# Seven-product matrix sets in a two-layer block: the weight sums of even and odd sets change engines, and two norm steps move

## The reference, cut to what matters

```
for l in range(2):
    n = rms_norm(h, mix_norm_g[l])
    proj = n @ w_in[l]                    # q, k, v, indexer, rnn, conv, gates
    ... attention, recurrent and convolution branches, merged ...
    h = h + merged @ w_out[l]
    f = rms_norm(h, ffn_norm_g[l])
    a = silu(f @ w_ffn_gate[l]) * (f @ w_ffn_up[l])     # width 2816 = 22 tiles of 128
    h = h + a @ w_ffn_down[l]
return h[:, 16:]
```

## Time and profile before

| | us |
|---|---|
| median of 3 runs | 1786.79 (1786.48 to 1790.79) |
| profiled execution | 1786.79 |
| its span | 1785.0 |
| TensorE busy | 1737.6 (97%) |
| VectorE busy | 953.5 (53%) |
| ScalarE busy | 492.0 (28%) |
| GpSimd busy | 326.7 (18%) |

### The profile page before, as it was taken

The page is one execution under the profiler, slowest core; times in us unless marked ns, Lnnn a source line. Parts: engine busy times, 40 slices in busy tenths (PEclk is TensorE's granted clock), DMA queues, the critical chain, the costliest instruction groups (busy, mean ns, idle before and its releaser), DMA issues.

```text
span 1785.0 us, 32239 instructions
## 1 busy us (share of the span) xinstructions
PE 1737.6 (97%) x13478; PEld 1442.2 (81%) x13478; DVE 953.5 (53%) x1921; ACT 492.0 (28%) x1064; POOL 326.7 (18%) x349
## 2 busy tenths in 40 slices
PE   6999998899899999999999999999999999999999
PEld 3345654898877888888889999988888888899999
DVE  2225335566456857566325765348667563257643
ACT  2122236344343124742102100051146322020100
POOL 0002300564100000000003555200000000036652
PEclk9999999799999999999999999999999999999999
DMA  8322300000234433332443444443334334444453
GB/s 326 121 94 95 118 24 1 3 4 4 95 145 142 142 142 133 127 127 109 142 141 142 166 166 154 158 161 142 142 135 145 122 118 142 152 155 168 171 170 107
DMA packets 53360, 225.46 MB, mean 126 GB/s; under 512 B 5088, under 2 KB 29024, under 8 KB 29280
## 3 DMA queue, kind: packets, MB, share of 16 engines
q1 hardware_dynamic: 53216, 223.40, 35.0%
HBM read 222.34 MB, written 1.05 MB: 125 GB/s over the span
## 4 chain that ended last, share of the span: by engine, by line
PE 93%; DVE 3%; ACT 2%; issue 1%; DMA 1%; DVEq 0%; SPq 0%; ACTq 0%
PE PS L535 26%; PE PS L730 14%; PE PS L676 13%; PE PS L1926 9%; PE PS L754 8%; PE PS L1423 2%; PE PS L1436 2%; PE PS L548 1%; PE PS L2024 1%; PE PS L649 1%; PE PS L694 1%; PE PS L688 1%; DMA ring<-stream_dram 1%; PE PS L618 1%; PE PS L630 1%
## 5 line engine op out<-in xcount | busy, mean ns | idle before, releaser
L535 PE MATMUL PS<-arena,ring 128*128 128x272 f32 (+1 forms) x2176 | 498.1, 389 | 0.0
L535 PEld LDWEIGHTS PS<-arena,ring 128*128 128x128 f32 x2176 | 411.2, 190 | 77.2 <-issue 1.4
L676 PE MATMUL PS<-arena,ring 128*128 128x272 f32 (+1 forms) x1024 | 229.5, 386 | 2.1 <-DVE arena L1210 2.1
L995 DVE SCALAR_TENSOR_TENSOR arena<-arena,par 128x272 f32<-128x272 f32 (+1 forms) x480 | 214.8, 488 | 16.7 <-issue 1.3
L676 PEld LDWEIGHTS PS<-arena,ring 128*128 128x128 f32 x1024 | 194.2, 190 | 36.0 <-DVE arena L1210 2.9
L954 POOL TENSOR_TENSOR arena<-ring 128x512 f32<-128x512 f32 (+1 forms) x32 | 39.9, 1246 | 978.0 <-PE PS L688 927.1
L1926 PE MATMUL PS<-arena,ring 128*128 128x512 f32 (+2 forms) x448 | 158.3, 514 | 1.7 <-DVEq L2241 1.7
L730 PE MATMUL PS<-arena 128*128 128x136 f32 (+1 forms) x1280 | 152.1, 277 | 0.0
L730 PEld LDWEIGHTS PS<-arena 128*128 128x128 f32 x1280 | 148.7, 191 | 0.0
L1926 PEld LDWEIGHTS PS<-arena,ring 128*128 128x128 f32 (+1 forms) x448 | 84.0, 189 | 75.1 <-issue 69.6
L769 ACT ACTIVATE arena<-PS 128x272 f32<-128x272 f32 (+1 forms) x144 | 55.5, 392 | 320.4 <-PE PS L535 313.9
(11 more groups left out here) (361 smaller groups left out, 2297.1 us busy)
## 6 DMA issues: line engine op xcount, KB each, us to landing
ring<-stream_dram SPq DMA_DIRECT2D x185, 1024.0 KB, 4.8
ring<-stream_dram SPq DMA_DIRECT2D x32, 512.0 KB, 4.3
ring<-stream_dram SPq DMA_DIRECT2D x16, 384.0 KB, 3.7
arena<-x_dram SPq DMA_DIRECT2D x1, 2048.0 KB, 11.4
cst<-const_dram SPq DMA_DIRECT2D x1, 1080.0 KB, 7.9
out_dram<-H SPq DMA_DIRECT2D x4, 256.0 KB, 3.4
cst<-const_dram SPq DMA_DIRECT2D x1, 912.0 KB, 9.6
arena<-stream_dram SPq DMA_DIRECT2D x1, 512.0 KB, 7.6
```

Of the source, the lines that this page charges most:

```text
L535: last = mm(PS[:, (m + f) % 4, nw], lslot(l, n, KD, 256)[:, k, P * f:P * f + P], NT[:, k, nw], start=k == 0, stop=k == KD - 1)
L676: last = mm(PS[:, i % 4, NQ], lslot(l, n, KD, 256)[:, k, P * (i % 2):P * (i % 2) + P], src[:, k, NQ], start=k == 0, stop=k == KD - 1)
L995: stt(CVG[:, c, NQ], CVA[:, c, j + Q0:j + T2], dw_w[l][:, c, j:j + 1], CVG[:, c, NQ], ALU.mult, ALU.add)
```

## The change

Three edits. First, in layer 1 (not in layer 0) the norm sum of the first norm is issued behind tile m = 0. Second, the seven `add_square` steps go, and one `add_tiles` (which waits for all eight squares) takes their place. Third, GpSimd and VectorE exchange their parts: VectorE makes the sums of the even sets, GpSimd those of the odd ones, each at the places in its list where its former sums stood.

```diff
                 if m == 0 and l == 0:
                     pe.wait_ge(fn_added, 1)
                     sum_parts(SQF, 4, slice(META, T2), fn_sums)
-                if m == 1:
+                if m == (0 if l else 1):
                     norm_sums(0, 5, NW)
...
-            def add_square(k):
-
-                dve.wait_ge(L["sq"], B["sq"] + KD + k + 1)
-                dr()
-                return tt(SQS[:, NQ], SQ2[:, 0, NQ] if k == 1 else SQS[:, NQ], SQ2[:, k, NQ], ALU.add)
...
                     tt(H[:, f, NQ], H[:, f, NQ], made, ALU.add).then_inc(L["br_kept"], 1)
-                    if f > 1:
-                        add_square(f - 1)
-            add_square(KD - 1).then_inc(L["added"], 1)
+            dve.wait_ge(L["sq"], B["sq"] + 2 * KD)
+            add_tiles(v, SQS[:, NQ], SQ2[:, :, NQ], SQ2[:, 0:4, NQ]).then_inc(L["added"], 1)
...
-            def odd_sums(j):
+            def even_sums(j):
...
-                weight_sums(v, quarters(l, FF_S + 2 + j), WS[j % 4]).then_inc(L["odd_sums"], 1)
+                weight_sums(v, quarters(l, FF_S + 2 + j), WS[j % 4]).then_inc(L["even_sums"], 1)
...
-            odd_sums(1)
+            even_sums(0)
             for j in range(QUADS):
...
                 if j % 2 == 0:
-                    odd_sums(j + 3)
+                    even_sums(j + 2)
...
-                for s in ((3, 5), (7,), (9, 11), ())[fp]:
-                    odd_sums(QUADS + s)
+                for s in ((2, 4), (6,), (8, 10), ())[fp]:
+                    even_sums(QUADS + s)
...
-            def even_sums(j):
+            def odd_sums(j):
...
-                weight_sums(g, quarters(l, FF_S + 2 + j), WS[j % 4]).then_inc(L["even_sums"], 1)
+                weight_sums(g, quarters(l, FF_S + 2 + j), WS[j % 4]).then_inc(L["odd_sums"], 1)
...
             for p in range(FT // 2):
-                even_sums(2 * p)
+                odd_sums(2 * p + 1)
...
-            for s in range(2, DOWNS, 2):
-                even_sums(QUADS + s)
+            for s in range(3, DOWNS, 2):
+                odd_sums(QUADS + s)
```

## The result

The changed kernel took 1807.7 us in the median of 5 runs (1799.0 to 1808.3), the kernel before 1786.79 (1783.04 to 1790.79). The ratio is 1.0102, with an interval of 1.0073 to 1.0131, which is 18.2 us (13.0 to 23.4); forecast were 16.9. The median itself lies 0.7 us above the upper end of the stated range. Run a second time, beside other kernels, the same code took 1801.81 us against 1786.85, ratio 1.0088 (1.0072 to 1.0103), which is 15.7 us (12.9 to 18.4).

What follows compares the result with a forecast made beforehand. TensorE, busy 97% of the span, was taken to bound the kernel. Waits of 2.65 + 4.68 + 5.06 = 12.4 us plus 4.5 us of slow clock on 1786.8 gave 1803.7 us; 8-of-10 range 1798.5 to 1807.

Steps and rivals of the forecast that it cites:

- Whatever newly makes TensorE wait is paid in full.: Rule for the whole kernel: new TensorE waits cost their full length; relieving other engines pays nothing unless TensorE waited for it.
- First norm of layer 1: At layer 1's start, TensorE waits 2.65 us for the squares' sum, and all of layer 1 starts that much later.
- the earlier root: In layer 1's first norm the root comes 0.8 us sooner, helping nobody: VectorE idles until ScalarE's swap.
- Squares: At the second norm the three-step sum exceeds its cover: 0.84 us of new waiting in layer 0, 0.88 in layer 1.
- Exchange, set 0: At set 0's third product TensorE waits for VectorE's late sums: 3.84 and 4.18 us, besides the second norm's 0.84 and 0.88.
- The 0.3 us allowed for this: Allowance, either way, for GpSimd's new sums of set 1 shifting VectorE's products: 0.3 us.
- Other sets: Sets after the first cost nothing: 1.4 us to spare in layer 1, 3.5 left in the down projection.
- The rival of late sums: VectorE late in every other set, each step waiting out a GpSimd step: 0.5 us in nine layer 1 sets, 1808.2 us; chance 0.11.
- Clock: Granted clock falls to half behind the three longest new waits: 1.6 us at each set 0, 1.3 at layer 1's start, together 4.5.
- A fall that was counted at 1.3: Clock fall behind the 2.65 us wait at layer 1's first norm, taken between two earlier cases: 1.3 us.
- The sum: Whole kernel: 12.4 us of waiting plus 4.5 us of slow clock, 16.9 us, giving 1803.7 us.
- Early sums cost nothing: Rival: set 0's sums run in VectorE's idle time before the root, 4.4 us in all, 1791.2 us; chance 0.05 with other no-cost ways.

Runs made afterwards that it cites:

- split wait: Kernel before, with the output projection's tile waiting for the last merged tile only at its eighth matmul: ratio 0.9993; same edit on the kernel with set 0 ahead: 1.0003.
- exchange alone: Kernel before with only the third edit, VectorE summing the even sets and GpSimd the odd: ratio 1.0085 (1.0066 to 1.0104).
- control: The changed kernel run again without any edit, against the kernel before: 1801.81 us, ratio 1.0088 (1.0072 to 1.0103).
- the kernel with set 1 later: The exchange alone, with GpSimd's sums for set 1 moved behind its first token sums: ratio 1.0032 (1.0020 to 1.0045) to the kernel before.
- the kernel with set 0 ahead: The exchange alone, with VectorE making set 0's sums before waiting for the second norm's root: ratio 0.9997 (0.9981 to 1.0014) to the kernel before.

## Why the prediction was right

Point by point, by its own steps; shifts are differences between the same loads of the two profiles.

- *"Whatever newly makes TensorE wait is paid in full."* Held to 0.3 us for every edit alone, the falls of the clock aside, and with the other sign for the split wait.
- *First norm of layer 1.* Forecast 2.65 us, measured a wait of 2.66 on the loads, and L562 2.5 us later. VectorE's idle time ahead of L1051 grew from 9.66 to 13.11 us, so the earlier root ended in an idle engine:

```profile
1197.06 1.23 DVE L1051 TENSOR_TENSOR arena<-arena 128x1024 f32<-128x1024 f32 x1 [13.11 <-ACT arena L801]
```

- *Squares.* Forecast 0.84 and 0.88, measured 0.81 and 0.83 of idle loads; the first up tile came 0.65 and 0.70 us later.
- *Exchange, set 0.* Forecast waits of 3.84 and 4.18 us, measured 4.05 and 4.39. The step was right, its size 0.2 short: beside GpSimd's token sums VectorE's four steps took what they had taken (0.68 to 0.96 us each), but VectorE's products ahead of them took 5.04 us in place of 4.67. The 0.3 us allowed for this was too small for the exchange alone, where it was 0.8.
- *Other sets.* Forecast 1.4 us to spare in set 4 of layer 1. Measured: sums end at 1628.69 + 0.69 = 1629.38, third product loaded at 1631.23, 1.85 to spare. In the changed kernel, VectorE and then the loads:

```profile
1623.84 1.42 DVE L954 TENSOR_TENSOR arena<-ring 128x512 f32<-128x512 f32 x1
1625.19 1.75 DVE L955 TENSOR_TENSOR arena<-ring 128x512 f32<-128x512 f32 x1
1627.02 1.60 DVE L957 TENSOR_TENSOR arena<-arena,ring 128x512 f32<-128x512 f32 x1
1628.69 0.69 DVE L959 TENSOR_TENSOR arena<-ring,arena 128x512 f32<-128x512 f32 x1
```

```profile
1631.23 0.86 PEld L730 LDWEIGHTS PS<-arena 128*128 128x128 f32 x7
```

  GpSimd's steps of the same time:

```profile
1623.45 1.27 POOL L955 TENSOR_TENSOR arena<-ring 128x512 f32<-128x512 f32 x1
1624.86 1.53 POOL L957 TENSOR_TENSOR arena<-arena,ring 128x512 f32<-128x512 f32 x1
1626.53 1.54 POOL L959 TENSOR_TENSOR arena<-ring,arena 128x512 f32<-128x512 f32 x1
```

  The rival of late sums was rightly rejected, but the prediction's reason for it, that VectorE is held up by less than a GpSimd step each time, needs a closer look. L954, L955 and L957 of VectorE end at 1625.26, 1626.94 and 1628.62, each 0.55 us behind the end of the GpSimd step during which it began (1624.72, 1626.39, 1628.07). So each is held until that step ends. The sum is 5.5 us and not 7.8 because each begins 0.3 to 0.5 us into the GpSimd step, so that less than a whole step is left to wait, and because the fourth, L959, met none and took 0.69.
- *Clock.* Forecast 4.5 us by three falls. In the profile there were two and no third; the same 2.3 us wait had one in three of the other kernels and none in the control. At set 0 both came each time. A fall that was counted at 1.3 stayed away, while the one at layer 1's set 0 lasted twice 3.41 us.
- *The sum.* Forecast 2.65 + 1.72 + 8.02 + 4.5 = 16.9 us. By the lengths of the parts the profile gives 2.5 for the first norm, 1.35 for the squares, 8.4 for the waits at set 0, 0.5 of restart behind them (the kernel with set 1 later, whose clock stayed up, shows 0.24 us a layer on top of its waits), for which the prediction had no term, and so 3.8 for the clock: 16.6. The mechanism was right, but that the totals lie 0.3 us apart is in part luck, as the waits came out longer and the norms and the clock cheaper.
- *Early sums cost nothing.* Rightly excluded for this kernel, and right as a mechanism, as the kernel with set 0 ahead shows.

## What to carry to other kernels

When two engines exchange alternate jobs, look at the first job of each list, not at the steady state: the steady state had room for the exchange in 31 of 32 sets, and the one job that lost an idle stretch to run in cost 13 us in two layers. Put work that an engine can do with what has already landed ahead of its next wait, and split a wait so that only the last matmul needs the last input. Where times scatter by more than the effect, compare the length between two fixed instructions of the profile.

## What the runs showed of the hardware

In these runs a VectorE add or product of two SBUF tiles that began during a GpSimd step of weight sums was held until that step ended; it wasn't slowed by a share. In the changed kernel's profile all 57 VectorE adds of 128x512 that began during a GpSimd step of weight sums ended 0.55 to 0.62 us behind its end, and those that met nothing on GpSimd took 0.68 to 0.69. It goes both ways: GpSimd's steps took 1.53 to 1.72 us where one of VectorE's sums was running at their start, and otherwise 1.26 to 1.32, but for one of 1.56 that began together with a VectorE product (955.28). So a product of 0.43 us can take 1.50, as in the exchange alone, and what it pays is what is left of the other engine's step.

The clock fell behind (or inside) each of the six waits of 4.05 to 4.95 us at set 0, in two profiles of the changed kernel and one of the exchange alone. It fell behind three of the five waits of 2.26 or 2.27 us at layer 1's start, and behind neither of the two of 2.5 us in the kernel with set 1 later. Filling a 4 us wait of TensorE with useless matmuls kept the clock at 1.00 (2.4 GHz), where the empty wait was followed by 3.41 us or more at about 0.5 (1.2 GHz), in both layers and in both profiles of the changed kernel.
